# One core, a two-block network in split fp32: embedding tiles on alternating bank pairs, two first tiles interleaved, recurrent openings reordered

## What is computed

```
# first block
h = rms_norm(x, norm_mix);  u_pool, q, k, v, g_a, g_b = split(h @ w_in)
merged = sigmoid(g_a) * (pool_mixer(u_pool) @ w_branch_a) + sigmoid(g_b) * (stick_breaking(q, k, v) @ w_branch_b)
x = x + merged @ w_out
h = rms_norm(x, norm_ffn);  x = x + (silu(h @ w_ffn_gate) * (h @ w_ffn_up)) @ w_ffn_down
gate = sigmoid(rms_norm(x, norm_ple) @ w_ple_gate)
x = x + gate * (p @ w_ple_proj)                     # the per-layer embedding, "PLE"
x = rms_norm(x, norm_final)
# second block
u = rmsnorm(x, g_pre_2)
feat_a, z_a, c_q, c_kv, k_pe, z_b, gate_logits = split(u @ w_in_2)
y_a = rwkv7_branch(feat_a, z_a)       # recurrent, 8 heads of 64
    # decay w = exp(-c * sigmoid(w0 + tanh(wd) @ w_decay_up)), rate a = sigmoid(a0 + ad @ w_iclr_up)
    # per token: S = S * w + (S @ -kk) (kk * a) + v k;  y = S @ r;  then group norm, gain, bias, silu(z)
y_b = mla_branch(c_q, c_kv, k_pe, z_b)            # latent attention, 8 heads
x = x + rmsnorm((g_a * y_a + g_b * y_b) @ w_o, g_post)
```

## Time and profile before

| | us |
|---|---|
| three runs | 2879.6, 2875.28, 2876.78 |
| median | 2876.78 |
| the profiled execution | 2879.11 |
| its span in the trace | 2877.3 |
| mean granted clock of TensorE | 0.981 of full speed |
| PE busy | 2706.5 (94 %) |
| DVE busy | 1334.2 (46 %) |
| POOL busy | 938.7 (33 %) |
| ACT busy | 679.6 (24 %) |

### The profile page before, as it was taken

One profiled execution on the slowest core, in us unless ns is written; L12 is line 12 of the kernel. 1 busy time (PEld: TensorE's weight loads), 2 busy tenths in 40 slices (PEclk: granted clock), 3 DMA queues, 4 the chain that ended last, 5 costly groups with the idle time before them and its releaser, 6 DMA issues. The chain is left out here.

```text
span 2877.3 us, 50264 instructions
## 1 busy us (share of the span) xinstructions
PE 2706.5 (94%) x21508; PEld 2116.9 (74%) x21508; DVE 1334.2 (46%) x1278; ACT 679.6 (24%) x949; POOL 938.7 (33%) x417
## 2 busy tenths in 40 slices
PE   7999999999999999999998889989899999998986
PEld 6677778887888888888876666666667777776765
DVE  7844442114523123212455754343556565543589
ACT  3433330001211000000132334443121212211331
POOL 4222214433444344444443221112112111224465
PEclk9999999999999999999999999999999999999998
DMA  3100001112111111111121200001011110113343
GB/s 126 37 30 30 29 15 50 45 51 102 44 51 44 51 51 44 51 44 51 51 73 66 81 22 15 22 15 61 32 36 42 38 47 31 49 49 111 118 158 103
DMA packets 40748, 156.15 MB, mean 54 GB/s; under 512 B 4640, under 2 KB 5152, under 8 KB 39200
## 3 DMA queue, kind: packets, MB, share of 16 engines
q1 hardware_dynamic: 31392, 110.21, 12.0%
q10 hardware_dynamic: 9216, 43.78, 4.1%
HBM read 133.00 MB, written 20.97 MB: 54 GB/s over the span
## 5 line engine op out<-in xcount | busy, mean ns | idle before, releaser
L2476 POOL TENSOR_TENSOR w_hi<-w_raw,one 128x1024 fp32r<-128x1024 f32 x199 | 386.7, 1943 | 1893.9 <-PE dps L285 1369.9
L285 PE MATMUL dps<-h_hi,w_hi 128*128 128x512 f32 x1744 | 557.3, 395 | 44.5 <-issue 11.1
L285 PE MATMUL dps<-h_lo,w_hi 128*128 128x512 f32 x1744 | 551.5, 392 | 0.0
L285 PE MATMUL dps<-h_hi,w_lo 128*128 128x512 f32 x1744 | 550.6, 391 | 0.0
L2478 POOL TENSOR_TENSOR w_lo<-w_raw,w_hi 128x1024 fp32r<-128x1024 f32 x199 | 523.7, 2632 | 15.6
L285 PEld LDWEIGHTS dps<-h_hi,w_hi 128*128 128x128 f32 x1744 | 328.3, 189 | 122.1 <-issue 35.8
L285 PEld LDWEIGHTS dps<-h_hi,w_lo 128*128 128x128 f32 x1744 | 329.8, 189 | 69.5
L285 PEld LDWEIGHTS dps<-h_lo,w_hi 128*128 128x128 f32 x1744 | 330.0, 189 | 69.0 <-issue 0.2
L302 PE MATMUL dps<-h_hi,w_hi 128*128 128x512 f32 x512 | 178.4, 420 | 16.4 <-ACT rw_sg L2093 7.9
L302 PE MATMUL dps<-h_lo,w_hi 128*128 128x512 f32 x512 | 174.9, 410 | 0.5 <-DVE rw_akt L2003 0.3
L302 PE MATMUL dps<-h_hi,w_lo 128*128 128x512 f32 x512 | 171.9, 414 | 1.2 <-DVE rw_akt L2003 1.1
(11 more groups left out here) (351 smaller groups left out, 3992.1 us busy)
## 6 DMA issues: line engine op xcount, KB each, us to landing
w_raw<-w_stream SPq DMA_DIRECT2D x200, 512.0 KB, 3.5
x_again<-x_t ACTq DMA_DIRECT2D x2, 4096.0 KB, 14.3
gates<-gate_out ACTq DMA_DIRECT2D x16, 512.0 KB, 2.7
tmp<-gates ACTq DMA_DIRECT2D x16, 512.0 KB, 4.3
x_t<-x_res ACTq DMA_DIRECT2D x4, 1024.0 KB, 4.0
out_t<-x_again SPq DMA_DIRECT2D x16, 256.0 KB, 2.0
back<-branches ACTq DMA_DIRECT2D x7, 512.0 KB, 7.6
x_res<-x_t ACTq DMA_DIRECT2D x2, 1536.0 KB, 12.5
```

Of the source, the lines that this page charges most:

```text
L285: mm = k.nc.tensor.matmul(k.dps[0:rows, pair, h * HALF:(h + 1) * HALF], w[:, slot, sub + t, 0:rows], x(t)[:, h * HALF:(h + 1) * HALF], sta ...
L2476: g.tensor_tensor(k.w_hi[:, s], k.w_raw[:, s], ones, ALU.mult).then_inc(k.sem("w_hi_done"), 1)
```

## The change

Five parts.

1. ACT carries out a Copy of one column (`first_use`) as soon as the constant `one` is set, ahead of the waits for x.
2. `out_pe` and `latent_pe` start with `split_pair`: k-steps 0 to 6 of tile 0, k-steps 0 to 6 of tile 1, then the last k-step of each. Only tile 0's k-steps wait for the splits of the activations.
3. In PLE the tile number decides the bank pair (t % 2), for gates and projections alike. Gate 0 is written as six k-steps, the norm's sums, two k-steps; ACT copies it out to `tmp0`, and DVE multiplies in place.
4. In the last halves of i = 0 to 2 the decay products stand right behind the `lt` products, ahead of the statistics; no fills stand ahead of the `l` products, and 12 stand at each of the next two places instead of 8 at three (`FILL_NEXT`). ACT carries out a Sigmoid of one column ahead of the wait for the decay products. The fills of `count.ahead` stand in front of `rk` instead of behind it.
5. In the first halves `gained` stands behind the t3 mask instead of ahead of it, and `gated`, `rate`, `floor`, `unit` and `kk` go one place or so later.

```diff
 def entry_act(k, act, x_t):
+    act.wait_ge(k.sem("one_done"), 1)
+    k.nc.scalar.activation(k.first_use[:, :], k.one[:, :], ACT.Copy, scale=k.one[:, :])
     act.wait_ge(k.sem("vec_loaded"), 16)
...
+def split_pair(k, pe, blk, slots, uses, ready, done=("blk_done", "blk_done"), freed=None):
+    last = lambda x: lambda t: x[:, KT - 1, :]
+    for j in range(2):
+        dense(k, pe, blk + j, slots[j], 0, rows(k.h_hi), rows(k.h_lo), KT - 1, j, uses[j], None, ready=ready if j == 0 else None, last=False)
+    for j in range(2):
+        dense(k, pe, blk + j, slots[j], KT - 1, last(k.h_hi), last(k.h_lo), 1, j, uses[j], done[j],
+              ready=(ready[0], ready[1] + KT - 1) if j == 0 else None, first=False)
...
 def out_pe(k, pe):
-              ready=("h_lo_done", KT) if j == 0 else None, freed=freed)
-    with pe.Fori(0, KT // 2 - 1) as i:
+    split_pair(k, pe, BLK["out"], (0, 1), (TILE["out"] // 2,) * 2, ("h_lo_done", KT))
+    with pe.Fori(1, KT // 2 - 1) as i:
...
+PLE_ORDER = [("gate", 0), *(("proj", n) for n in range(4)), *(("gate", n) for n in range(1, 5)), *(("proj", n) for n in range(4, 8)),
+             *(("gate", n) for n in range(5, 8))]
+PLE = {tile: (t % 2, TILE["ple"] // 2 + t // 2) for t, tile in enumerate(PLE_ORDER)}
...
 def ple_pe(k, pe):
+            if n == 0:
+                dense(k, pe, at, slot, 0, rows(k.h_hi), rows(k.h_lo), 6, pair, use, None, ready=("h_lo_done", 3 * KT), last=False)
+                stat(k, pe, 2)
+                dense(k, pe, at, slot, 6, later(k.h_hi), later(k.h_lo), 2, pair, use, "blk_done", ready=("h_lo_done", 3 * KT + 6), first=False)
...
 def ple_dve(k, dve):
-        v.tensor_tensor(k.tmp[n % 2][:, :], k.dps[:, 0, :], k.inv[:, :], ALU.mult).then_inc(k.sem("pair0_out"), 1)
+        if n == 0:
+            ple_wait(k, dve, ("gate", 0))
+            v.tensor_tensor(k.tmp0[:, :], k.tmp0[:, :], k.inv[:, :], ALU.mult).then_inc(k.sem("ple_first_done"), 1)
...
+            v.tensor_tensor(k.tmp[n % 2][:, :], k.dps[:, pair, :], k.inv[:, :], ALU.mult).then_inc(k.sem(f"pair{pair}_out"), 1)
...
 def ple_act(k, act, p_t, x1_t, pos_t):
+    a.activation(k.tmp0[:, :], k.dps[:, PLE["gate", 0][0], :], ACT.Copy).then_inc(k.sem(f"pair{PLE['gate', 0][0]}_out"), 1)
...
 def latent_pe(k, pe):
-    dense(k, pe, b, 0, 0, rows(k.h_hi), rows(k.h_lo), KT, 0, LATENT_USE, "blk_done", ready=("h_lo_done", 4 * KT))
+    split_pair(k, pe, b, (0, 1), (LATENT_USE,) * 2, ("h_lo_done", 4 * KT))
     next_stat(k, pe)
-    dense(k, pe, b + 1, 1, 0, rows(k.h_hi), rows(k.h_lo), KT, 1, LATENT_USE, "blk_done")
...
-        after = {} if end else {DECAY_AT: lambda: rw_decay_pe(k, pe, i + 1), NORM_AT: lambda: rw_norm_pe(k, pe, i + 1)}
-        rw_half_pe(k, pe, last, first, LAST_NAMES[i], after, FILL_LONG)
+        rw_half_pe(k, pe, last, first, LAST_NAMES[i], {} if end else {NORM_AT: lambda: rw_norm_pe(k, pe, i + 1)}, FILL_LONG if end else FILL_NEXT,
+                   None if end else lambda: rw_decay_pe(k, pe, i + 1))
...
+FILL_NEXT = Fill(0, 12, 9, 9, 9, 24, 3)
...
+    fill(count.ahead)
     u.wait(pe, AHEAD, "rk")
...
-    fill(count.ahead)
...
+    if opening is not None:
+        opening()
     if before is not None:
         rw_result_pe(k, pe, before, "mean")
-    fill(count.masks - 1)
+    fill(count.masks - 1 if opening is None else 0)
...
-        "t2": result(before, "rstd3") + setup(last, "l"), "x2": result(before, "normed", "gained"),
-        "t3": result(before, "summed", "gated"), "x3": setup(last, "rate", "floor"),
+        "t2": result(before, "rstd3") + setup(last, "l"), "x2": result(before, "normed"),
+        "t3": result(before, "gained", "summed"), "x3": result(before, "gated"),
...
 def rw_decay_act(k, act, i, w_up):
+        a.activation(k.first_use[:, :], k.zero[:, :], ACT.Sigmoid)
```

More of the change, by code:

```diff
@@ L975, with ple_wait @@
 PROJ_AT = (1, 6)
-def ple_pe(k, pe):
-    b, use = BLK["ple"], TILE["ple"] // 2
-    for n in range(KT):
-        dense(k, pe, b + GATE_AT[n], GATE_AT[n] % 2, 0, rows(k.h_hi), rows(k.h_lo), KT, 0, use + n, "blk_done",
-              ready=("h_lo_done", 3 * KT) if n == 0 else None, freed="ple_h_free" if n == KT - 1 else None)
-        if n == 0:
-            stat(k, pe, 2)
-        if n % 4 == 0:
+PLE_ORDER = [("gate", 0), *(("proj", n) for n in range(4)), *(("gate", n) for n in range(1, 5)), *(("proj", n) for n in range(4, 8)),
+             *(("gate", n) for n in range(5, 8))]
+PLE = {tile: (t % 2, TILE["ple"] // 2 + t // 2) for t, tile in enumerate(PLE_ORDER)}
+def ple_wait(k, engine, tile):
+    pair, use = PLE[tile]
+    engine.wait_ge(k.sem(f"pair{pair}_out"), use + 2)
+def ple_pe(k, pe):
+    b = BLK["ple"]
+    later = lambda x: lambda t: x[:, t + 6, :]
+    for kind, n in PLE_ORDER:
+        pair, use = PLE[kind, n]
+        if kind == "gate":
+            at, slot = b + GATE_AT[n], GATE_AT[n] % 2
+            if n == 0:
+                dense(k, pe, at, slot, 0, rows(k.h_hi), rows(k.h_lo), 6, pair, use, None, ready=("h_lo_done", 3 * KT), last=False)
+                stat(k, pe, 2)
+                dense(k, pe, at, slot, 6, later(k.h_hi), later(k.h_lo), 2, pair, use, "blk_done", ready=("h_lo_done", 3 * KT + 6), first=False)
+            else:
+                dense(k, pe, at, slot, 0, rows(k.h_hi), rows(k.h_lo), KT, pair, use, "blk_done", freed="ple_h_free" if n == KT - 1 else None)
+        else:
             at = PROJ_AT[n // 4]
-            for j in range(4):
-                dense(k, pe, b + at, at % 2, 2 * j, rows(k.p_hi), rows(k.p_lo), 2, 1, use + n + j,
-                      "blk_done" if j == 3 else "ple_proj_done", ready=("p_lo_done", 0) if n + j == 0 else None)
+            dense(k, pe, b + at, at % 2, 2 * (n % 4), rows(k.p_hi), rows(k.p_lo), 2, pair, use,
+                  "blk_done" if n % 4 == 3 else "ple_proj_done", ready=("p_lo_done", 0) if n == 0 else None)
 def ple_dve(k, dve):
     v = k.nc.vector
-    b, use = BLK["ple"], TILE["ple"] // 2
+    b = BLK["ple"]
     g = VEC["norm_final"], VEC["g_pre"]
@@ L1045, in keep @@
             act.wait_ge(k.sem("ple_x_done"), n - 3)
-        a.activation(k.p_proj[:, n % 4, :], k.dps[:, 1, :], ACT.Copy).then_inc(k.sem("pair1_out"), 1)
+        pair = PLE["proj", n][0]
+        a.activation(k.p_proj[:, n % 4, :], k.dps[:, pair, :], ACT.Copy).then_inc(k.sem(f"pair{pair}_out"), 1)
     def sigmoid(n):
-        act.wait_ge(k.sem("pair0_out"), use + n + 2)
+        if n == 0:
+            act.wait_ge(k.sem("ple_first_done"), 1)
+        else:
+            ple_wait(k, act, ("gate", n))
         a.activation(k.tmp[n % 2][:, :], k.tmp[n % 2][:, :], ACT.Sigmoid).then_inc(k.sem("ple_gate_done"), 1)
@@ L1617, with rw_half_pe @@
 FILL_LONG = Fill(0, 8, 9, 9, 9, 24, 3)
-def rw_half_pe(k, pe, u, before, tiles, inserted, count):
+FILL_NEXT = Fill(0, 12, 9, 9, 9, 24, 3)
+def rw_half_pe(k, pe, u, before, tiles, inserted, count, opening=None):
     product = k.sem("rw_product")
@@ L1685, in rw_half_pe @@
     b.then_inc(product, 1)
+    if opening is not None:
+        opening()
     if before is not None:
         rw_result_pe(k, pe, before, "mean")
-    fill(count.masks - 1)
+    fill(count.masks - 1 if opening is None else 0)
     free("l")
     free("kkp_tm")
-    fill(1)
+    fill(1 if opening is None else 0)
     for c in range(NC):
@@ L1883, in rw_pair_dve @@
         "t1": result(before, "rstd0", "rstd1"), "x1": result(before, "rstd2"),
[L1884 to L1887 removed]
+        "t2": result(before, "rstd3") + setup(last, "l"), "x2": result(before, "normed"),
+        "t3": result(before, "gained", "summed"), "x3": result(before, "gated"),
+        "t4": setup(last, "rate", "floor", "unit0"), "x4": setup(last, "unit1"),
+        "t5": setup(last, "unit2", "unit3"), "x5": setup(last, "kk", "b", "k") + ahead(last, "rp", "kkp", "bq", "kq"),
         "turned": ahead(last, "rk") + [z_take]})
```

18 lines of the change are left out of this document (10 added, 8 removed).

## The result

The changed kernel takes 2858.23 us in the median (2855.64 to 2858.95), the kernel before, run beside it, 2878.19 (2875.28 to 2879.69). The ratio is 0.993, with a 95 % interval of 0.9918 to 0.9942: 20 us less, where 27.8 less and 2849 were forecast, 2841 to 2860 as the range. The profiled execution took 2857.92 (span 2856.1), 21.2 less than that of before. One execution of the kernel with the entry's change alone took 4714.59 us, at a mean granted clock of 0.691, and is left out of that kernel's ratio.

The account below looks back on a forecast made before the run. PE, busy 2706.5 of 2877.3 us, was taken as the bound, so only its waits matter. Terms -5.6 + 15.6 + 13.5 + 4.9 - 0.6 = 27.8 us less gave 2849.0, with 8 in 10 between 2841 and 2860.

Parts of the forecast that it names:

- rival C: PLE: contention lengthens DVE's 10.37 us chain per gate back to 12.5, so 8.2 us come back: 2857; chance 0.09.
- PLE: Gates and projections: with bank pairs in turn, PE's waits for emptied banks go, 17.2 us less up to gate 7.
- Openings: Last halves of head pairs 0 to 2: lt to state products takes 12.7 instead of 17.19 us, 13.5 less in all.
- Rival D: Openings: another table is in ACT when `rw_sg` comes, so the preload fails and fills wait: 2851 to 2856; chance 0.05.
- First halves of pairs 1 and 2: Recurrent part: moving `gained` removes two `rw_t` waits, 3.3 us, plus 1.6 for a lowered clock: 4.9 less.
- Output projection: Its first tiles: POOL's split for tile 2 comes late, PE stands 3.4 us, lowered clock adds 2.2: cost 5.6.
- Rival A: Output projection: the split is hidden, because k-steps or hand-over run other than reckoned: 5.6 us better, 2843; chance 0.09.
- Latents: Latent tiles behind PLE, to tile b+3: 1.6 us lost; sums come earlier, but PE idles about 9 us for `pe_raw`.
- rival B: Latent tile 0: the clock falls where PE is busy 1.36 of each 1.74 us; about 5 us stay: 2854; chance 0.10.
- First half of pair 0: Recurrent part: fills ahead of `rk` cost 0.6 us; moving `rate`, `floor` and `kk` one slot later costs 0.
- Rival E: Short first halves: moved DVE steps meet POOL's splits, PE standing 3.1 us in each of nine slots: slower; chance 0.02.
- Entry: Kernel start: the small Copy moves ACT's first table load earlier; PE's start gains 0, bounds 0 and 1.3 us.

## Why the prediction came out as it did

The direction and the range were right, and so was the mechanism at every place but the first half of head pair 0; the size was 28 forecast for 20 measured (21.2 in the profiled executions). The measured 2858.2 lies 1.8 us inside the slow end of the range, where the prediction had only C (2857, 0.09), which did not come, and a mixture of smaller misses (2857 to 2871, 0.02), which did. That it stayed inside is in part luck, since misses of both signs cancel below. Term by term:

- **PLE**, 17.2: measured 17.2, and 17.2 alone. The step that mattered, DVE's chain of 10.37 us within a period of 10.9, held; rival C did not come.
- **Openings**, 13.5: measured 13.0, and 13.1 alone. The bound from pair 3's opening plus eight matmuls, 12.7, was 12.74. The slack for `rw_sg` was 0.9 us rather than 0.7. Rival D is out: the load stood at 2089.95 and `rw_sg` began without one.
- **First halves of pairs 1 and 2**, 4.9: measured 5.5, confirmed by taking the list back (5.4).
- **Output projection**, -5.6: measured -3.5. The stall of 3.4 was 3.17; the mis-sized term is the lowered clock behind it, 2.2 by my choice. It ran at 1.00 from 689.7 to 696.5. My own bound of 3.0 had left it out. Rival A, that the split is hidden, is out.
- **Latents**, -1.6 behind PLE: measured -3.0 to tile b+3. From the sums to the start of tile b+2 it was 14.4 us, for 14.3 reckoned; but the sums started 0.7 later than reckoned, and the clock stayed down for 5.71 us and cost 2.9 instead of 2.2. The clock did not fall in tile b (rival B): it was 1.00 from 1613 to 1623 and 0.51 from 1623.1 to 1627, in the wait for `pe_raw`.
- **First half of pair 0**, -0.6: measured -5.9. This is the step that failed. The prediction said that `rate` and `floor` "go one slot later" and priced that at 0, because the products that need them come late enough. That was the wrong question: what comes behind them on DVE are the x4 masks, and PE waits for those. Rival E had the mechanism (a moved step that meets a split), but as nine places or none, with 3.1 us each; it happened at one, with two steps in a row and 3.15 us. I had argued from the low mean of `gained` and had not looked at where POOL's split stands beside the t4 mask in pair 0. In the trace of before that mask ends at 2065.87 and the split begins at 2065.66, so it lies over the very slot into which the steps were moved. Together with 1.7 us for the clock this is 4.9 of the 5.3 missed. The rest of the 5.9 stands at the opening of this half: the `lt` products come 2.2 us later (PE waits 8.02 us for `rw_v` where it waited 6.79 for `rw_rkv`, and runs 5.4 us at 0.50 behind it where it ran some 3), and 0.8 of it comes back when the next wait, for `rw_xm`, falls from 1.37 to 0.52, and 0.5 in the last part of the half.
- **Fills ahead of rk**, -0.6: not resolved. Taking them back moved the `lt` products by 0.3 us, and the other way.
- **Entry**, 0: 1.2 us earlier at PE's start, near the end of the bound of 1.3, in the main by contention (0.86 in the run with the entry alone) and not by the load's own length.
- **The end**, 0: 2.8 us lost, behind the recurrent part, where nothing was changed. The stretches of lowered clock fell differently. This is not a cost of an edit: with only the pair 0 list undone the end gave 2.5 us back.

So of the 6.6 us between 27.8 and 21.2, 5.3 are the first half of pair 0, 2.8 the end, 1.9 the latents and what lies behind them, 0.5 the openings; 2.1 at the output projection, 1.2 at the entry and 0.6 in pairs 1 and 2 go the other way.
